# Two weight splits ahead of the logarithms, and three steps moved to a later place, in the heads of a gated DeltaNet layer

## The reference

```
proj = hn @ w_in                                   # 2048 -> 12352 columns
qkv = silu(causal_depthwise_conv(qkv, conv_w))     # four taps per channel
q = l2_normalize(q) * 128**-0.5; k = l2_normalize(k)     # 16 key heads of 128
beta = sigmoid(b); g = -exp(a_log) * softplus(a + dt_bias)
gc = cumsum(g); decay = where(causal, exp(gc_i - gc_j), 0)     # in chunks of 64 tokens
m = where(strict, (k * beta) @ k.T * decay, 0)
t_inv = inverse(eye + m)
u = t_inv @ (v * beta); w = t_inv @ (k * beta * exp(gc))
# over the chunks: v_new = u - w @ S; o = qg @ S + qk @ v_new; S = S * exp(g_last) + kd.T @ v_new
o = rms_norm(o, o_norm) * silu(z);  mix = o @ w_out
```

## Time and profile before

| | us |
|---|---|
| median of 3 runs | 3643.78 (3641.04 to 3651.09) |
| the profiled execution | 3639.94 |
| its span, first to last instruction | 3638.3 |
| PE busy | 3339.0 (92%) |
| DVE busy | 2427.0 (67%) |
| ACT busy | 1800.0 (49%) |
| POOL busy | 712.8 (20%) |

### The profile page before, as it was taken

The page is one execution under the profiler, slowest core; times in us unless marked ns, Lnnn a source line. Parts: engine busy times, 40 slices in busy tenths (PEclk is TensorE's granted clock), DMA queues, the critical chain, the costliest instruction groups (busy, mean ns, idle before and its releaser), DMA issues.

```text
span 3638.3 us, 60991 instructions
## 1 busy us (share of the span) xinstructions
PE 3339.0 (92%) x19058; PEld 2817.2 (77%) x19058; DVE 2427.0 (67%) x4397; ACT 1800.0 (49%) x3770; POOL 712.8 (20%) x969
## 2 busy tenths in 40 slices
PE   6898898999989999999999878777999999999986
PEld 5787777888878888888888654444888888888875
DVE  4788888766655577457755459988557755775544
ACT  4555455555554455445544345555545544454433
POOL 0888888400000000000000015554000000000000
PEclk7999999999999999999999988888999999999998
DMA  4434344444436766666666452212566666666643
GB/s 130 117 110 123 109 116 117 113 113 109 118 102 190 192 183 191 185 184 181 188 176 163 117 149 76 74 51 82 161 175 180 184 184 190 182 193 167 184 113 104
DMA packets 1003986, 525.29 MB, mean 144 GB/s; under 512 B 34448, under 2 KB 998032, under 8 KB 1003392
## 3 DMA queue, kind: packets, MB, share of 16 engines
q1 hardware_dynamic: 998080, 507.06, 50.5%
q0 software_dynamic: 5824, 17.21, 1.5%
HBM read 511.61 MB, written 12.62 MB: 144 GB/s over the span
## 4 chain that ended last, share of the span: by engine, by line
PE 68%; DVE 14%; ACT 7%; issue 6%; DMA 3%; SPq 1%; POOL 0%; ACTq 0%; DVEq 0%; POOLq 0%
PE bank L260 38%; PE bank L261 19%; PE bank L563 4%; DVE w_lo L248 3%; DMA raw<-in_ple_w_gate_dram 2%; DVE y L1464 2%; ACT w_hi L242 1%; ACT L833 1%; ACT rot L833 1%; PE bank L303 1%; ACT T L833 1%; DVE x L1681 1%; DVE y L1461 1%; DVE rb L1727 1%; ACT tiles L833 1%
## 5 line engine op out<-in xcount | busy, mean ns | idle before, releaser
L260 PE MATMUL bank<-act,w_hi 128*128 128x512 f32 x4352 | 1617.0, 412 | 28.1 <-DVE w_lo L248 22.7
L248 DVE TENSOR_TENSOR w_lo<-raw,w_hi 128x512 fp32r<-128x512 f32 x1856 | 1233.7, 715 | 306.6 <-ACT w_hi L242 300.8
L261 PE MATMUL bank<-act,w_lo 128*128 128x256 f32 x4352 | 1230.4, 283 | 0.0
L260 PE MATMUL bank<-mid,w_hi 128*128 128x512 f32 x3072 | 1098.2, 402 | 23.3 <-DVE mid L1641 12.6
L242 ACT ACTIVATE w_hi<-raw 128x512 fp32r<-128x512 f32 x1856 | 1042.7, 619 | 151.8 <-DMA raw<-in_ple_w_gate_dram 66.8
L260 PEld LDWEIGHTS bank<-act,w_hi 128*128 128x128 f32 x4352 | 833.6, 192 | 245.8 <-DVE w_lo L248 33.6
L261 PE MATMUL bank<-mid,w_lo 128*128 128x256 f32 x3072 | 861.8, 281 | 0.0
L261 PEld LDWEIGHTS bank<-act,w_lo 128*128 128x128 f32 x4352 | 837.3, 192 | 5.0 <-issue 3.6
L260 PEld LDWEIGHTS bank<-mid,w_hi 128*128 128x128 f32 x3072 | 580.5, 189 | 164.2 <-DVE mid L1641 13.8
L261 PEld LDWEIGHTS bank<-mid,w_lo 128*128 128x128 f32 x3072 | 583.0, 190 | 1.6
L270 ACT ACTIVATE tiles<-bank 128x256 f32<-128x256 f32 x384 | 145.4, 379 | 640.8 <-PE bank L261 640.8
(11 more groups left out here) (264 smaller groups left out, 3242.4 us busy)
## 6 DMA issues: line engine op xcount, KB each, us to landing
raw<-in_mlp_w_up_dram SPq DMA_DIRECT2D x128, 1024.0 KB, 6.3
raw<-in_mlp_w_down_dram SPq DMA_DIRECT2D x128, 1024.0 KB, 5.9
raw<-in_gdn_w_in_dram SPq DMA_DIRECT2D x96, 1024.0 KB, 5.8
raw<-in_gdn_w_out_dram SPq DMA_DIRECT2D x32, 1024.0 KB, 6.2
raw<-in_ple_w_gate_dram SPq DMA_DIRECT2D x32, 1024.0 KB, 5.9
raw<-in_s_w_out_dram SPq DMA_DIRECT2D x32, 1024.0 KB, 6.3
raw<-in_s_w_in_dram SPq DMA_DIRECT2D x16, 1024.0 KB, 6.4
turns_scratch<-tiles POOLq DMA_DIRECT2D x64, 128.0 KB, 2.3
```

The lines of the kernel that those rows point to most:

```text
L248: eng.tensor_tensor(w_lo[par][:, c], raw[slot][:, c], w_hi[par][:, c].bitcast(F32), ALU.subtract).then_inc(S("lo_ready"), 1)
L260: eng.matmul(a[:, :], w_hi[par][:, w], rhs[:, k0 + kt, :], start=(k0 + kt == 0), stop=False)
L261: mm = eng.matmul(a[:, 0:NT], w_lo[par][:, w], rhs[:, k0 + kt, 0:NT], start=False, stop=(k0 + kt == kend - 1))
```

## The change

Four moves, all in the order of calls; no operation is added or dropped.

- ACT, steps 17 to 19: the three splits of these steps stand together ahead of the tanh of z and of the logarithms and exponentials (before, the splits of steps 18 and 19 stood behind them).
- PE: `key_products(r + 1)` after step 21, not 20.
- DVE: `key_matrix(r + 1)` in step 21, not 20, and so behind the low half of step 21; the convolution of y[2] in step 22, not 21.
- ACT and DVE: tanh and gate of y[2] in step 1 of the head that uses it (behind ACT's copy of P2, and behind DVE's L1, ahead of `take` of the next tile). Before, tanh was in step 22 of the head before, and the gate at the end of its step 23. For the first head they move out of the loop over the first four chunks.

```
@@ PE, head
                     core(r, s)
-                    if s == 20 and not last:
+                    if s == 21 and not last:
                         key_products(r + 1)
@@ ACT, first four chunks
-                if n < 3:
+                if n < 2:
                     gate_tanh(n, n % 2, y[:, n, :], "conv_done", n + 1, n < 2)
@@ ACT, around
+                elif s == 1:
+                    gate_tanh(n + 2, 0, y[:, 2, :], "conv_done", 4 * r + 3)
...
-                elif s == 22:
-                    gate_tanh(n + 8, 0, y[:, 2, :], "conv_done", 4 * r + 7)
@@ ACT, head
                 for s in range(24):
-                    if s < 8 or not last:
-                        c, q = s // 4, s % 4
+                    ahead = {17: (17, 18, 19), 18: (), 19: ()}
+                    for s_ in ahead.get(s, (s,)):
+                        if s_ >= 8 and last:
+                            continue
+                        c, q = s_ // 4, s_ % 4
@@ DVE, around
                 if s == 1:
+                    gate(n + 2, 0, y[:, 2, :])
                     take(n + 3, 3)
...
                 elif s == 20:
                     take(n + 8, 2)
+                elif s == 21:
                     key_matrix(r + 1)
-                elif s == 21:
+                elif s == 22:
                     conv(r + 1, n + 8, 2)
@@ DVE, head
                     around(r, s, last)
-                    if s == 23 and not last:
-                        gate(6 * r + 8, 0, y[:, 2, :])
```

## The result

| | before | after |
|---|---|---|
| median | 3647.4 us of 4 (3641.0 to 3651.4) | 3587.0 us of 4 (3584.5 to 3601.1) |
| span of the profiled execution | 3638.3 | 3586.0 |
| first product behind the heads (PE, on mid) | 1082.1 | 1021.8 |
| the rest of the span, whose code is the same | 2556.2 | 2564.2 |

The ratio is 0.9849, with a 95% interval from 0.9831 to 0.9868: 55 us faster, 48 to 62. Forecast were 52.6 and 3591. In the two profiled executions the heads end 60.3 us earlier; 8.0 of that is lost again behind them. The heads are where to look, and they repeat.

A forecast was written before the change was run, and what follows sets the result against it. TensorE, busy 92% of the span, was taken as the bound, so only idle and half-clock time could be won. Nine heads at 4.1, six at 2.4 and 1.3 make 52.6: 3643.8 - 52.6 = 3591 us, range 3573 to 3613.

The forecast's parts named there:

- The early splits bring qkn 3.3 us forward and end the stall: Head change beside POOL: DVE starts unit_qk at 483.8 instead of 487.06, so PE's 3.29 us wait for qkn goes.
- Key products a quarter later: PE reaches the key products some 1.4 us later, at 486.4, with qkn there at 485.0; P keeps 0.7 us margin.
- PT comes in time: Head change beside POOL: with tanh of y behind the copy of P2, PE's 1.7 us stall goes if P is in time.
- A new wait of 2.2 us for RT, and 0.4 behind it: PE at DVE's RT add beside POOL: 2.6 us taken from a gain of 6.7, net 4.1 a head.
- Half clock gone: PE's clock at head changes beside POOL: the 1.2 GHz stretch goes with the qkn stall, 1.7 us a head.
- rival B: Head changes beside POOL: the new wait keeps the half clock, 2.4 us gained a head, 37 in all, 3607; chance 0.18.
- After POOL 2.4 us a head: Six head changes after POOL: stalls of 1.5 and 0.8 plus 0.1 of pipeline refill go, 14.4 us together.
- POOL ends at about the same time: End of POOL's work: hardly moves, now in mid-head, sparing one head the L1553 wait of 1.3 us.
- The other DVE waits stay, less 1.3 us: Rest of the heads: nothing gained, except one head's L1553 wait of 1.3 us.
- C: Heads beside POOL: POOL sets their time, so only the short changes gain, 14.4 and 1.3 us, 3628; chance 0.07.
- D: Heads beside POOL: denser DVE meets POOL at all times, w_lo slows, kernel 18 us slower, 3662; chance 0.04.
- A: Head changes beside POOL: DVE is quick, no new wait for RT, 6.7 us a head, 76 in all, 3568; chance 0.11.

The follow-up runs named there:

- S alone: Kernel before with only the splits of steps 18 and 19 moved forward to stand with that of step 17: 3605.1 us, ratio 0.9899.
- S and G: Changed kernel with key products and key matrix put back in step 20, early splits and moved tanh and gate of y[2] kept: 3597.5 us, ratio 0.9880.
- G: Kernel before with only tanh and gate of y[2] moved to step 1: 3634.4 us, ratio 0.9967.
- K alone: Kernel before with only key products, key matrix and the convolution of y[2] one step later: 3681.9 us, ratio 1.0113.
- G and K: Kernel before with tanh and gate of y[2] in step 1 and the later key products, key matrix and convolution, without early splits: 3630.8 us, ratio 0.9955.
- POOL laid around: Changed kernel with POOL held to four turns a head, three from step 2 on, the fourth behind step 14: 3548.6 us, ratio 0.9740.

## Why the prediction was right, by its own steps

- *The early splits bring qkn 3.3 us forward and end the stall.* Right: DVE's idle time fell from 5.24 to 1.91 us, the 29.2 and 9.1 us of the earlier trace rows are gone, and S alone earns 37 of the 55 us by the ratios, 42 of 60 by the medians.
- *Key products a quarter later.* The stall had gone without it (S and G have no wait for qkn). P is ready 0.8 us before PE turns it (0.7 foretold). But the margin is of use only with G there; K alone costs 1.1%. The prediction saw the margin and not the second chain over ACT's tanh.
- *PT comes in time.* Right: 13.9 and 3.8 us gone. Alone it would be worth 0.3%.
- *A new wait of 2.2 us for RT, and 0.4 behind it.* Measured 1.7 and 0.5 in each head beside POOL, none after it. The best of the working: 2.6 foretold, 2.2 found; DVE takes 12.9 us from qkn to RT, where the working had 14.0.
- *Half clock gone.* Partly wrong: it stayed in four of ten heads, at 1.0 us each. That is rival B in part; B priced it at 1.7 in all nine. B's premise that a stall of 1.7 us leaves the clock alone does not hold either: stalls of 1.70 and 0.46 us brought it down in those four.
- *After POOL 2.4 us a head.* Measured 58.13 - 55.35 = 2.8. The two stalls are 2.3 of it; the rest is PE's busy time, 55.84 a head before and 55.35 after the earlier trace rows. The 0.1 of refill in the sum stands in no row; that the 0.5 is refill was not shown.
- *POOL ends at about the same time.* Wrong. Its last store moved from 687.41 to 721.45, and a tenth change of heads lies beside it. A turn took 9.3 us in the mean with DVE busy for 84%, and 9.9 with 90%. First before, then after:

```profile
687.41 0.58 POOL L1252 DMA_DIRECT2D turns_scratch<-tiles  x1 [0.65 <-POOL tiles L1250]
...
721.45 0.58 POOL L1255 DMA_DIRECT2D turns_scratch<-tiles  x1 [0.65 <-POOL tiles L1253]
```

- *The other DVE waits stay, less 1.3 us.* Too small. The wait for L1553 (DVE's copy of the second half of v_new, called VN) fell from 10.7 us to 3.5, and this one, which the prediction had not listed, went:

```profile
PE bank L561 <- DVE RT L1535: 4.5, 8, 0.7
```

PE's terms over all sixteen heads: qkn -38.3, PT -18.9 (19.7 to 0.8), L673 -6.6 (11.0 to 4.4), L561 -4.5, RT and P2T +21.5 (15.2 + 4.2 in nine heads, 2.1 in the tenth), w_lo +0.8, half clock 9 x 1.7 less 4 x 1.0 = -11.3. Together -57.3 of the 60.3; the other 3.0 us stand in no row of waits. The forecast had -52.6: right in its large terms, and short by the two DVE waits in mid-head.

That the sum came so close is in part luck. Up to the ninth change of heads the prediction had 9 x 4.1 = 36.9 us, and 46.9 were found: 2.3 in the first head and 5.6 in each of the next eight, above its own 3 to 5. What lies behind gave 13.4 where 15.7 were foretold. And the two profiled executions differ by 52.3 us, nearly the 52.6 foretold, only because 8.0 of the heads' 60.3 were lost again in code that is the same; the medians differ by 60.4, and the ratio gives 55.

The median w_lo beside POOL, as in the earlier trace rows:

```profile
L248 DVE TENSOR_TENSOR w_lo<-raw,w_hi x217: 677/955/1217, 160.9 to 695.1; 128x512 fp32r<-128x512 f32 x109
```

Of the rivals, C (POOL holds the pace at 65.0) fell at once, though POOL and the heads do run in step (below), as did D: the median w_lo went from 898 to 955 ns, far from 1.14 us. A had its mechanism right, as the kernels without POOL's arithmetic and with POOL laid around show, but the change itself doesn't take POOL out of the way. The Trainium skill (GPSIMD Engine Reference, 1. Specifications) states that GpSimd's SBUF interfaces are shared with VectorE; the trace agrees, in w_lo (955 ns beside POOL, 685 after it) and in the wait for RT, 1.7 us a head with POOL's arithmetic and none without. These runs show the slowing, not the interface.

## What to carry to other kernels

Price a move by the chain that ends last behind it, on every engine queue that it crosses, and not by the stall that it removes: here the kernel with G and K, with nearly half of PE's wait for qkn, its wait for PT and all but one stretch of half clock removed, was no faster beside POOL. Test moves in combination; one that costs 1.1% alone can cost nothing behind another. And look where a helper engine's background work lies: two waits in POOL's queue, with nothing left out, earned a further 1.1%.

## What was not expected of the hardware

- Heads and POOL's turns fall into step by themselves. Before, seven turns to a head of 65.0 us; after, six to a head, in 59.0 or 60.0 us, and again so with POOL started 7.5 us later. Each is slower beside the other (w_lo 685 to 955 ns; a turn 9.3 to 9.9 us with the denser DVE); what draws them into step was not tried. In S alone and in S and G the heads keep varying (60.7 to 62.9 and 59.9 to 64.6 us).
- The granted clock does not follow the length of a stall alone. A mean stall of 3.2 us brought 1.2 GHz in all nine heads before; stalls of 1.70 and 0.46 us brought it in four of ten after; in G and K, stalls of 3.0 us for RT with 1.8 and 1.2 us ahead of them left one low stretch in nine heads. What decides it was not found.
